# Two more weight slots for the experts, places that turn slot by slot, and tokens picked one pass ahead

## The reference

```python
grp = jnp.argmax(g_logits, axis=-1)                       # one of 4 groups
top_v, top_i = lax.top_k(e_in_grp, TOP_K)                 # 2 of its 8 experts
weights = (jax.nn.softmax(top_v, axis=-1) * p_grp).reshape(n_asg)
expert = (grp[:, None] * EXPERTS_PER_GROUP + top_i).reshape(n_asg)
...
gate, up = jnp.split(xb @ w_gate_up[e], 2, axis=-1)       # 1024 x 1024
return (jax.nn.silu(gate) * up) @ w_down[e]               # 512 x 1024
```

## Time and profile before

| | |
|---|---|
| Time before | 1663.04 us, median of 3 runs (1661.64 to 1663.22) |
| Span of the profiled execution | 1661.7 us |
| PE busy | 1534.3 us (92%) |
| DVE busy | 1005.3 us (60%) |
| ACT busy | 679.3 us (41%) |
| DMA | 421.05 MB, mean 253 GB/s |
| Granted TensorE clock, mean | 0.97 of full speed |

### The profile page before, as it was taken

The page is one execution under the profiler, slowest core; times in us unless marked ns, Lnnn a source line. Parts: engine busy times, 40 slices in busy tenths (PEclk is TensorE's granted clock), DMA queues, the critical chain, the costliest instruction groups (busy, mean ns, idle before and its releaser), DMA issues.

```text
span 1661.7 us, 30547 instructions
## 1 busy us (share of the span) xinstructions
PE 1534.3 (92%) x12376; PEld 1275.5 (77%) x12377; DVE 1005.3 (60%) x1756; ACT 679.3 (41%) x986; POOL 361.5 (22%) x223
## 2 busy tenths in 40 slices
PE   9999987777777767999999999999999999999998
PEld 8889974444444334788889998888888899988887
DVE  5875732222221222888758678866788658788854
ACT  6464421111111001555535755544454436655542
POOL 1120040000000000154203614430344107324410
PEclk9999998898988888999999999999999999999999
DMA  8545699999999999654545465445554545465450
GB/s 350 199 173 208 242 374 430 431 431 434 432 432 433 434 431 428 244 189 172 179 160 179 157 224 189 174 176 208 191 189 167 179 157 197 153 218 191 168 184 26
DMA packets 37284, 421.05 MB, mean 253 GB/s; under 512 B 4330, under 2 KB 6522, under 8 KB 9154
## 3 DMA queue, kind: packets, MB, share of 16 engines
q1 hardware_dynamic: 36514, 415.49, 64.5%
q0 software_dynamic: 672, 4.15, 0.6%
HBM read 416.45 MB, written 3.18 MB: 253 GB/s over the span
## 4 chain that ended last, share of the span: by engine, by line
PE 82%; DMA 11%; DVE 3%; issue 2%; ACT 1%; ACTq 1%; SPq 0%; DVEq 0%
PE bank L1276 19%; PE bank L1293 10%; PE bank L1278 10%; DMA ring<-moe_w_dram 8%; PE bank L785 7%; PE bank L787 6%; PE bank L786 6%; PE bank L1164 6%; PE bank L1295 5%; PE bank L1193 3%; DMA area<-moe_w_dram 2%; PE bank L1099 2%; DVE sq L2523 1%; DMA ring<-first_w_dram 1%; PE bank L1376 1%
## 5 line engine op out<-in xcount | busy, mean ns | idle before, releaser
L1276 PE MATMUL bank<-h_split,w_hi 128*128 128x512 f32 x1408 | 489.7, 392 | 0.6 <-DVE h_split L2109 0.6
L1276 PEld LDWEIGHTS bank<-h_split,w_hi 128*128 128x128 f32 x1408 | 264.3, 188 | 59.6 <-DVE h_split L2109 1.2
L1761 ACT CAST w_hi<-ring 128x2048 fp32r<-128x2048 f32 (+2 forms) x124 | 232.8, 1879 | 146.0 <-PE bank L1295 102.7
L680 POOL TENSOR_TENSOR area<-area,stat 128x256 f32<-128x256 f32 x88 | 215.3, 2447 | 293.9 <-DVE area L2600 293.9
L1278 PE MATMUL bank<-h_split,lo_last 128*128 128x256 f32 x840 | 234.8, 280 | 0.0
L2118 DVE TENSOR_TENSOR lo_last<-ring,w_hi 128x2048 fp32r<-128x2048 f32 (+3 forms) x75 | 174.2, 2325 | 7.2 <-ACT w_hi L1761 7.1
L1278 PE MATMUL bank<-h_split,lo_first 128*128 128x256 f32 x568 | 158.8, 280 | 0.0
L1278 PEld LDWEIGHTS bank<-h_split,lo_last 128*128 128x128 f32 x840 | 157.7, 188 | 0.0
L1164 PE MATMUL bank<-ring,sq 128*32 128x256 f32 x1408 | 112.5, 484 | 43.1 <-DVE sq L2523 33.1
L1164 PEld LDWEIGHTS bank<-ring,sq 128*32 128x32 f32 x1408 | 63.6, 137 | 86.0 <-issue 75.4
L2118 DVE TENSOR_TENSOR lo_first<-ring,w_hi 128x2048 fp32r<-128x2048 f32 (+3 forms) x50 | 116.8, 2335 | 2.8 <-ACT w_hi L1761 2.8
(11 more groups left out here) (482 smaller groups left out, 3457.7 us busy)
## 6 DMA issues: line engine op xcount, KB each, us to landing
ring<-moe_w_dram SPq DMA_DIRECT2D x38, 3072.0 KB, 32.4
ring<-layer_w_dram SPq DMA_DIRECT2D x56, 1536.0 KB, 6.7
area<-moe_w_dram SPq DMA_DIRECT2D x18, 3072.0 KB, 31.7
ring<-layer_w_dram SPq DMA_DIRECT2D x32, 1408.0 KB, 6.4
ring<-layer_w_dram SPq DMA_DIRECT2D x34, 1024.0 KB, 5.2
ring<-first_w_dram SPq DMA_DIRECT2D x21, 1536.0 KB, 6.9
ring<-moe_w_dram SPq DMA_DIRECT2D x12, 1536.0 KB, 12.5
area<-moe_w_dram SPq DMA_DIRECT2D x4, 1536.0 KB, 10.0
```

Source lines behind the costliest of these rows:

```text
L680: pool.tensor_tensor(up, up, stat[:, 3, :], ALU.mult).then_inc(S("up_scaled"), 1)
L1276: pe.matmul(halves(first_bank + side), hi_of(q)[:, cols], h_split[:, :, k, :], start=k == 0, stop=False, skip_group_check=True)
L1761: act.copy(hi_of(q)[:, cols], ring[:, PLACES[q % len(PLACES)], cols]).then_inc(S("hi_a_ready"), 1)
```

## The change

- Two more slots, each used once. The *early* slot has room of its own in SBUF (the memory that the framework keeps for descriptors of POOL's DMAs goes from its default to 4096 bytes per partition); it takes the first expert's slot 0 during the first stage, behind its twelfth piece. The *late* slot lies over `h_t` and `probs_t`, which the router has read when `logits_done` is 2; it takes slot 13. So 14 slots are ordered ahead.
- `moe_w` is one slot per row; each of the twelve other places is refilled by itself, behind the semaphore of the slot that it held before, in the order `TURNING`. Each place has a semaphore of its own, and PE waits for each slot. The last slot comes in three pieces of 1024 numbers per partition, each with its semaphore.
- In a pass PE picks the tokens of the next pass (`pick_tokens`) behind the products with gate and up, and turns them (`turn_tokens`) ahead of down; the hidden values are turned ahead of `combine`. The first pick is done ahead of the loops, and after the last pass one is picked that nobody uses.
- ACT and DVE loop over all passes. For each pass DVE reads the expert and the passes before it from a new table, `plan`, which is made once by three products on PE, a comparison on DVE and a copy on ACT. DVE makes the picking matrix of pass n + 1 ahead of the shares of pass n.
- The fifth slot of the first layer no longer waits for `moe_done`, since the last expert lies in `area`.
- The semaphores of the first stage's bounds and of two tables are merged.

```diff
+TURNING = (0, 1, *AREA_PLACES, 3, 6, 4, 2, 5, 7)
+FIRST_PLACES = (EARLY_PLACE, *TURNING, LATE_PLACE)
+def moe_before(s):
+    return s - len(TURNING) - (s < MOE_PLACES + len(TURNING))
...
+                if n == FIRST_SLOTS // 2:
+                    fill(0)
                 if n == FIRST_SLOTS - 5:
                     sp.wait_ge(S("level_done"), 4)
-                    fill(RING)
-                    fill(RING + 1)
+                    fill(3)
+                    fill(4)
...
-            for m, n in ((0, 18), (1, 19), (5, 19), (2, 20), (6, 20), (4, 21), (7, 21)):
+            for s, n in ((1, 18), (2, 19), (7, 19), (8, 20), (9, 20), (10, 21), (11, 21)):
                 first_slot_used(sp, n)
-                fill(m)
+                fill(s)
             sp.wait_ge(S("logits_done"), 2)
-            fill(3)
+            fill(12)
+            fill(13)
...
-            def refill(done, held, source, pairs=EXPERT_PAIRS):
-
-                before = passes_until(done)
-                for i in range(pairs):
-                    sp.wait_ge(S(EXPERT_SLOT_USED[2 * i + 1]), before)
-                    pair = EXPERT_PAIRS * held + i
-                    sp.dma_start(moe_pair(pair), source(i)).then_inc(pair_full[pair], 16)
-                return before
...
+            def refill(slots, done, source):
+
+                for s in slots:
+                    of, i = divmod(moe_before(s), EXPERT_SLOTS)
+                    if s == slots[0] or i == 0:
+                        before = passes_until(done(of))
+                    sp.wait_ge(S(EXPERT_SLOT_USED[i]), before)
+                    place = moe_place(s)
+                    if s < MOE_SLOTS - 1:
+                        sp.dma_start(moe_slot(place), source(s)).then_inc(moe_full[place], 16)
+                        continue
+                    for (landed, _), at in zip(last_parts, range(0, SLOT, D)):
+                        sp.dma_start(moe_slot(place)[:, at:at + D], source(s)[:, at:at + D]).then_inc(landed, 16)
...
-                if q == len(PLACES) - 1:
-                    sp.wait_ge(S("moe_done"), 1)
-                elif q >= len(PLACES):
+                if q >= len(PLACES):
                     slot_consumed(sp, q - len(PLACES))
...
+            def expert_pass(nth, e, turn, passes_end=None):
+
                 for k in range(KB):
...
                 m.then_inc(S("up_done"), 1)
...
+                pe.wait_ge(S("share_t_ready"), nth)
+                pick_tokens(nth + 1)
+
+                pe.wait_ge(S("hid_ready"), nth)
+                settled(pe)
+                pe.transpose(ps[1][:, 0:P], two["hid"], ident).then_inc(S("hid_turned"), 1)
 
                 pe.wait_ge(S("y_ready"), nth)
                 settled(pe)
                 combine(False)
                 pe.wait_ge(S("share_ready"), nth)
+                pe.wait_ge(S("picked_ready"), nth + 1)
                 settled(pe)
...
                 pe.wait_ge(S("hid_t_ready"), nth)
                 settled(pe)
+                turn_tokens()
+
                 for k in range(4):
...
+            pick_tokens(1)
+            pe.wait_ge(S("spread_copied"), 1)
+            keep_clock(1, 1)
+            pe.wait_ge(S("planned"), 3)
+            pe.matmul(ps[3][0:1, 408:408 + PASSES + 1], ones[0:EXPERTS - 1, 0:1], ended[0:EXPERTS - 1, :],
+                      start=True, stop=True)
+            pe.matmul(ps[3][0:1, 457:457 + PASSES + 1], passes_of[:, 0:1], ended, start=True, stop=True)\
+                .then_inc(S("planned"), 1)
...
+            copy_picked(1)
+            act.wait_ge(S("planned"), 4)
+            act.copy(plan[0:1, :], ps[3][0:1, 408:408 + 2 * (PASSES + 1)]).then_inc(S("planned"), 1)
...
+            with dve.Fori(1, total_passes(packed)) as n:
+                selected(*planned(n + 1))
+                shared(*planned(n))
+                hidden(n + 1)
+                picked_moved(n + 2)
```

More of the change, by code:

```diff
@@ L490, in program, with total_passes, moe_slot @@
         layer_full = [S(f"layer_full{i}") for i in range(len(PLACES))]
[L491 to L503, removed]
+        own_landed = [S(f"own_landed{i}") for i in range(3)]
+        third_landed = layer_full[0], layer_full[4], own_landed[0]
+        moe_full = {place: layer_full[PLACES.index(place)] if place in PLACES else S(f"moe_full{place}")
+                    for place in TURNING}
+        moe_full |= {EARLY_PLACE: own_landed[0], LATE_PLACE: own_landed[1]}
+        landed_before = {place: FIRST_FULL[PLACES.index(place)] if place in PLACES else int(place == EARLY_PLACE)
+                         for place in FIRST_PLACES}
+        last_parts = (own_landed[0], 3), (own_landed[1], 2), (own_landed[2], 1)
+        def total_passes(packed):
+            return nc.s_assert_within(packed // 16 + packed % 16, EXPERTS, PASSES,
+                                      skip_runtime_bounds_check_because="T tokens have TOP_K experts each")
+        def moe_slot(place):
+            if place == EARLY_PLACE:
+                return early_slot[:, :]
+            if place == LATE_PLACE:
+                return late_slot[:, :]
+            at = (place - RING) * SLOT
+            return ring[:, place, :] if place < RING else area[:, at:at + SLOT]
         diff_stat = ffs[:, 3, 0, :]
@@ new lines, in _ @@
+            first_in_loop = MOE_PLACES + len(TURNING) + 2
+            whole = (MOE_SLOTS - first_in_loop) // len(TURNING)
+            refill(range(MOE_PLACES, first_in_loop), lambda e: e, lambda s: moe_w[s])
+            with sp.Fori(0, whole) as turn:
+                refill(range(first_in_loop, first_in_loop + len(TURNING)), lambda e: e + EXPERT_SETS * turn,
+                       lambda s: slot_of(moe_w, s + len(TURNING) * turn))
+            refill(range(first_in_loop + len(TURNING) * whole, MOE_SLOTS), lambda e: e, lambda s: moe_w[s])
@@ L1160, in expert_pass @@
                         settled(pe)
-                    weights = expert_weights(held, k * D, rounds, last)
+                    weights = expert_weights(e, k * D, turn)
                     tokens = picked_t[:, k % 2, k // 2 * WIN:(k // 2 + 1) * WIN]
@@ L1182, in expert_pass @@
                 m.then_inc(S("share_turned"), 1)
-                pe.wait_ge(S("hid_ready"), nth)
-                settled(pe)
-                pe.transpose(ps[1][:, 0:P], two["hid"], ident).then_inc(S("hid_turned"), 1)
                 pe.wait_ge(S("hid_t_ready"), nth)
                 settled(pe)
+                turn_tokens()
                 for k in range(4):
-                    weights = expert_weights(held, (KB + k) * D, rounds, last)
+                    weights = expert_weights(e, (KB + k) * D, turn)
                     tokens = two["hid_t"][:, k * WIN:(k + 1) * WIN]
@@ L1197, in expert_pass, with expert @@
                 m.then_inc(S("down_done"), 1)
-            def expert(turn, held, last=False):
-                packed = pe.value_load(meta[0:1, bass.ds(EXPERT_SETS * turn + held, 1)], min_val=1,
+            def expert(e, turn=0):
+                packed = pe.value_load(meta[0:1, bass.ds(EXPERT_SETS * turn + e, 1)], min_val=1,
                                        max_val=16 * (EXPERTS + ASSIGNED // WIN) + WINDOWS)
@@ L2493, in _ @@
             for choice, where in enumerate((e1, e2)):
-                own.mark(tt(where, over(const("expert"), TT), over(best_at[:, :, choice], EXPERTS, 2), ALU.is_equal))
+                own.mark(tt(where, over(const("count")[:, 0:EXPERTS], TT), over(best_at[:, :, choice], EXPERTS, 2), ALU.is_equal))
             own.wait()
@@ L2568, in _, with planned @@
-            with dve.Fori(1, EXPERTS) as e:
-                expert(e)
+            dve.wait_ge(S("tables_moved"), 16)
+            selected(0, 0)
+            dve.wait_ge(S("planned"), 2)
+            ts(ended, const("count", EXPERTS), ps[3][0:EXPERTS, 400:401], None, ALU.is_ge).then_inc(S("planned"), 1)
+            picked_moved(1)
+            def planned(n):
+                e = dve.value_load(plan[0:1, bass.ds(n, 1)], min_val=0, max_val=EXPERTS - 1)
+                before = dve.value_load(plan[0:1, bass.ds(n + PASSES + 1, 1)], min_val=0, max_val=PASSES)
+                first = nc.s_assert_within((n - before) * P, 0, (WINDOWS - 1) * P,
+                                           skip_runtime_bounds_check_because="an expert has at most T tokens")
+                return e, first
```

183 lines of the change are left out of this document (86 added, 97 removed).

## The result

The changed kernel takes 1671.06 us (median of 5 runs, 1668.13 to 1674.73), the kernel before beside it 1663.22 (5 runs, 1661.64 to 1666.7): a ratio of 1.0043, interval 1.0028 to 1.0058, so 7 us slower. Forecast were 1659.5, and 1654.0 to 1664.5 as the range. The result lies outside it, on the other side of no change.

The account below looks back on a forecast made before the run. Weight DMAs were taken to bound the experts' stage, its end set by the last slot's landing at 663.6 us; -3.4 (landing) - 0.3 (tail) + 0.2 (layers' first slots) = -3.5, so 1663.0 becomes 1659.5 us, range 1654.0 to 1664.5.

Parts of the forecast that it names:

- the diff changes nothing that it waits for: In the layers, after the experts' stage: PE is at 9 tenths and its waits are unchanged; no term in us.
- the sum: Whole kernel: -3.4 (last landing) - 0.3 + 0.2 (tail and layers' first slots) = -3.5 us, giving 1659.5 us.
- Something outside the stage moves: A sign of being wrong: something outside the experts' stage changes; given no size and no chance.
- rival 3: Refills in the experts' stage: a fixed cost for each transfer, 3.74 us a slot, time 1667.5 us; chance 0.10.
- Singles, 3.67 us a slot: Experts' refills: 110 slots come singly instead of in 55 pairs, at 3.67 us a slot in place of 3.635.
- The gap at the start, 0.5 us (0 to 1.7): Start of refilling: slot 15's issue barely beats the queue's end, 0.5 us lost, between 0 and 1.7.
- The last landing, 660.2: End of the experts' stage: last weight slot lands at 660.2 us, 3.4 before 663.6.
- Two slots ahead: Start of the experts' refills: two slots ordered ahead and the DMA engines' dry time together worth 8 us.
- The tail: From last landing to down's end: 2.8 us instead of 3.6; 0.5 (0 to 2) added for low clock; gain 0.3.
- The pass: Middle of the experts' stage: picking a pass ahead is worth nothing, since PE waits for weights.
- Rival 4: Experts' passes: a new wait (table reads, loop jumps) binds; one microsecond over 14.5 on 31 passes makes 1690; chance 0.03.
- The first stage: Before the experts: the early slot fits into DMA gaps at no cost, up to 2 us if the lead were gone.

Follow-up runs that it names:

- before_area32: The kernel before with 32 unused bytes ahead of the area alone, which moves `h_split` and what lies behind it; 1670.31 us, ratio 1.0034.
- after_again: The changed kernel run once more with no edit; 1671.1 us, ratio 1.0043 to the kernel before.
- after_aligned: The changed kernel with 448 unused bytes ahead of the ring, so that it starts on a multiple of 512; 1667.82 us, ratio 1.0026.
- after_both: The changed kernel with the ring on a multiple of 512 bytes and the area 32 past a multiple of 64; 1667.33 us, ratio 1.0018.
- after_area: The changed kernel with the ring at byte 10240 and five small tables behind the area, so `h_split` starts as in the kernel before; 1662.43 us, ratio 0.999.
- after_two_pads: The changed kernel with two unused tensors: ring on a multiple of 512 bytes, `h_split` 160 past one; 1661.39 us, ratio 0.9983.
- after: The changed kernel as it is, beside the kernel before; 1671.06 us, ratio 1.0043.
- after_12: `after_both` without the early and the late slot: 12 places, singles, last slot in three pieces; 1672.01 us, ratio 1.0041 to the kernel before.
- before_singles: The kernel before with each of the 55 pair refills issued as two DMAs of 1536 KB; 1665.62 us, ratio 1.0009.

## Why the prediction was wrong, point by point

**The step that failed** is the sentence that from the first product of the layers on "the diff changes nothing that it waits for", and with it the sum, which has no term for anything outside the stage. True of the waits, and not enough. The layers took 4.0 and 4.6 us more in the two profiled executions of the changed kernel, and in `before_area32` 7.3 more for 32 bytes. The diff itself showed the tensors of SBUF moving, and I priced none of it, not even with a bound. "Something outside the stage moves" stands among the signs of being wrong, without a chance. No rival held it either: rival 3 came out near the right time (1667.5) for another reason, a fixed cost for each single.

**Singles, 3.67 us a slot.** Right as a price of singles, wrong for this kernel. From slot 16's landing (255.7) to slot 126's (661.6), 110 slots, it took 3.69 us a slot, in `after_again` 3.70. With the ring on a multiple of 512: 3.66 (`after_aligned`), 3.67 (`after_both`, `after_area`, `after_two_pads`). The start of the ring costs 0.02 to 0.03 us a slot, 2 to 3 us in the stage. The landings (issue plus time to landing) between 270 and 655 us tell which slots pay. In the six kernels of singles whose ring starts on a multiple, a slot of the ring lands 3.64 us after the one before it, a slot of `area`, which starts on such a multiple in no kernel, 3.68 (medians). With the ring 64 bytes past, in `after` and `after_again`, both take 3.69. Within a kernel the rows in HBM are alike for both, so it is the place written to that costs. A rule of the Trainium skill fits its direction ("DMA: Bandwidth & Descriptors", section "How a descriptor splits into AXI transactions"): a descriptor that doesn't start on a multiple of 256 bytes takes its first bytes from the boundary below, and so one transaction more. For a row of 12288 bytes, if it is one descriptor, that would be 49 for 48, an estimate of 2%; the trace shows 3.69 against 3.64 us, 1.4%. The page tells of reads, and the traces show the written side; no run tells 256 from 512.

**The gap at the start, 0.5 us (0 to 1.7).** Too small. I took slot 15 for the critical one and 2 us for an issue to move bytes. Slot 14 was issued when forecast, 1.3 us later with the whole first stage, yet by slot 16's landing 3.4 us were lost. What is lost goes with the time from the issue of slot 14 to the landing of the late slot, which is the queue's end (the last column: slot 16's landing from the end of the first stage):

| kernel | issue of 14 | late slot landed | between | 16 landed | lost (less 3 x 3.67) | 16, from first stage |
|---|---|---|---|---|---|---|
| after_two_pads | 235.8 | 242.8 | 7.0 | 253.8 | 0.0 | 32.7 |
| after_both | 236.2 | 241.8 | 5.6 | 254.2 | 1.4 | 32.6 |
| after | 238.5 | 241.3 | 2.8 | 255.7 | 3.4 | 32.3 |
| after_again | 239.6 | 242.3 | 2.7 | 256.6 | 3.3 | 32.2 |
| after_area | 237.6 | 240.2 | 2.6 | 255.1 | 3.9 | 32.6 |
| after_aligned | 238.4 | 240.9 | 2.5 | 255.7 | 3.8 | 32.1 |

One run with 7.0 us between lost nothing, one with 5.6 lost 1.4; 2 us are not enough. But the last column is nearly the same in all six, where 30.9 was forecast: a queue that ends later loses less, and slot 16 lands no sooner for it. So the gap alone explains no difference between these kernels. Why PE's first products and the queue's end stand differently to each other in kernels with the same work isn't settled.

**The last landing, 660.2, from the first stage's end on 438.4.** In the changed kernel 442.0: +2.9 for the gap, +2.2 for 3.69 in place of 3.67, -1.5 because the late slot came at 241.3 and not at 242.8 (a slot behind the forecast 237.5, and the first stage's 1.6), together 3.6. With both starts mended it is 440.0 (`after_area`) and 440.4 (`after_two_pads`): of the 3.4 us forecast 1.7 and 1.3 came. The slots behind the sixteenth kept the forecast 3.67 there; the sixteenth itself landed 1.7 and 1.8 us later than forecast.

**Two slots ahead.** Right in its direction, too large in its size: 8 us were forecast in the last landing, and `after_12` against `after_both` gives 2.7. They differ already when slot 15 lands, by 2.8, counted from the end of the first stage. The dry time explains half of it: `after_12` lost 2.8 us there (four slots in 17.5 us where 4 x 3.67 = 14.7 would do), less than the 4.2 lost before, and `after_both` still lost 1.4. The other half is the slot more that has landed: it should have been worth 3.67, but the thirteenth slot of `after_both` landed 16.5 us after the first stage, the twelfth of `after_12` 14.3. The order of the places differs between the two as well, and its part wasn't tested.

**The tail.** Forecast 2.8 us from the last landing to down's end, with 0 to 2 us in it for the lower clock. Measured 2.3 in `after`, but 3.6 in `after_again`, and 2.2 to 4.0 in all kernels with the new pass. Where it was 3.6 and more (`after_again`, `after_area`, `after_two_pads`, `after_12`), the last up blocks or the pick behind them took 1.82 to 1.97 us in place of 1.07. So the mechanism and its bounds hold, and that `after` came near 2.8 is luck.

**The pass.** No wait for ACT or DVE took the place of another. Before, PE stood most for their copies, 74.8 us in all, and for weights only 14.2; after, it waits for weights alone, 109.1 us. So what the new order takes out of PE's path comes back as waits for weights, as forecast. What PE waited for from 300 to 650 us (engine, line, releaser, us, times, longest), before and after:

```profile
PE bank L1164 <- DVE sq L2523: 38.4, 25, 1.6
PE bank L1151 <- ACT area L1725: 21.7, 25, 1.0
PE bank L1193 <- DVE sq L2535: 14.7, 25, 0.6
PE bank L1164 <- DMA ring<-moe_w_dram: 9.5, 7, 2.6
PE bank L1164 <- DMA area<-moe_w_dram: 4.7, 3, 2.7
```

```profile
PE bank L1183 <- DMA ring<-moe_w_dram: 79.9, 46, 2.2
...
PE bank L1183 <- DMA area<-moe_w_dram: 29.2, 17, 2.2
```

Rival 4 is out. No run changes the pass alone, so its share of the 2.8 us isn't known.

**The first stage.** It was taken as unchanged; it ended 1.6 and 2.6 us later in the changed kernel and between 0.7 earlier and 1.8 later in the seven changed kernels whose ring was mended. Its weights go through the ring too, but the spread of the mended kernels is as large as the effect: how much of it is the ring's start stays open.

**The sum, with what was measured.** 1661.7 + 1.6 (first stage) - 1.1 (experts) + 0.2 + 4.0 (layers) = 1666.4, the span to 0.1. For `after_again`, whose profiled execution (1671.52 us) is near the median: 1661.7 + 2.6 + 0.9 + 4.6 = 1669.8 (span 1669.7). With the two starts mended the change gives -2.8 us by the ratio (1.0 to 4.7), where -3.5 was forecast; part of that agreement is luck, since the landing gained less than forecast and the tail was longer, and the first stage of that execution was 0.7 us shorter.

**What stays open.** `h_split` at 160 or 224 past a multiple of 512 gave 5.55 us a group, at 96 5.60, at 64 and 192 5.65, at 128 5.58 in the first layer and 5.65 in the second, with the same operands. That the place within 512 bytes decides fits the groups of all fourteen kernels, but the only two starts with the same place, 204448 and 205472, lie 1024 bytes apart, so a place within 1024 bytes would fit as well. Nor do the groups give the whole loss: at 96 the layers took 978.3 and 978.4 us, at 64, with the slower groups, 977.8. I can't say by what mechanism it works, and a pad of any kernel has to be tried. The pads also move other tensors that lie behind the area, `hid_own` among them, and none was moved without `h_split`, so that `h_split` is the tensor that matters is the likeliest reading, not shown.

## What to carry to other kernels

A diff that adds, drops or resizes a tensor moves all that are allocated behind it, and in a kernel at the limit of an engine that can be worth more than the change: compare the starts of the hot tensors and the duration of one and the same instruction far from the change, and try a pad. Times by stage show a gain and a loss that cancel in the whole. A queue stays full only by what is issued well ahead of its end (here 7.0 us was enough and 5.6 was not), but filling it gains only what the landings behind it gain. And read the tail from more than one execution: the clock made it 2.2 to 4.0 us in kernels with the same work.

## What the runs showed of the hardware

- With the place of `h_split` and what lies behind it, the time of an fp32 product of 512 columns went from 392 to 397 ns at the same clock, without a wait. 32 bytes made a kernel 0.34% slower (971.8 to 979.1 us in the layers), 64 bytes another 0.3% faster (978.4 to 971.8).
- Slots written to a ring that starts 64 bytes past a multiple of 512 came at 426 GB/s as singles of 1536 KB, and at 430 on a multiple; pairs of 3072 KB at 431 and 432 to 433. In one and the same kernel slots of the aligned ring took 3.64 us each, those of the unaligned `area` 3.68. The DMA engines read as fully busy in all.
- A slot issued 2.5 to 2.8 us before the queue's last landing left 3.3 to 3.9 us unused, one issued 5.6 us before it 1.4, one issued 7.0 us before it none.
- With singles in the full queue an issue on SP took longer. In `after` the longest with eight DMAs or fewer under way took 0.8 us and most 0.33; with ten the median was 3.0 and the longest 6.9. Pairs, with as long a time to landing (38.8 us at most) but half as many DMAs, stayed at 0.35 or less. DMA didn't slow from it: 430 GB/s in `before_singles`, where most issues took 0.33, and in `after_both`, where the median was 3.0.
